# Three reorderings in a fused two-layer decoder step: an exponential step against its consumer, a projection column against a pair of transposes, a copy against a square

## The chip, the cores and the metric

The kernel runs on one NeuronCore of a Trainium2 chip. The metric is the device time of one execution in microseconds, as a median over executions. The engines are TensorE (PE: matmuls; PEld: its weight loads), VectorE (DVE), ScalarE (ACT), GpSimd (POOL) and SyncE (SP, which issues most transfers). Each works through its own instructions in order; between engines only semaphores order the work.

## The reference

One step of a two-layer decoder trunk for a prompt of 256 tokens and 8 samples of 4 tokens (288 columns in all, model width 1024), in float32. The three places that the change touches compute this:

```
# layer 0, Mamba-2 scan, chunks of 128 tokens
a_cs = cumsum(dt * A);  decay_in = exp(where(causal, a_cs[q] - a_cs[k], -inf))
y_diag = einsum(C.B, decay_in, x*dt);  y_off = einsum(C, h_prev, exp(a_cs))
y = (y_diag + y_off + x * d_skip) * silu(z)
# layer 1, RWKV-7 mixer
r, k, v = xr @ wr, xk @ wk, xv @ wv
kk = k * kk_coef;  kk = kk / max(sqrt(sum(kk*kk)), 1e-12)      # per head of 64
S = S * w_t + (S a_t) b_t^T + v_t k_t^T;  y_t = S r_t           # here in chunks, by a triangular inverse
```

Around them lie the attention of layer 0, its feed-forward part, and the mixture of experts of layer 1 (8 experts, top 2).

## The kernel before

Activations lie feature-major, as 8 tiles of 128 features by 288 tokens. Each engine has its program written out by hand; weights stream through a ring of three slots, which SP fills again when the last reader has signalled. The eight PSUM banks are dealt out in the order of `stage` calls: stage number modulo 8 is the bank, and a bank is taken again when its last reader has signalled `bank_free`. Two lists set the order of the work, and all engines walk over the same list: `first` (calls of `l0`, from line 418) for the layer-0 mixer, and `core` (calls of `step`, from line 531) for the RWKV core. Each engine does its own share of an item and passes over items in which it has none.

**Items of `first` around the change.** The 16 heads of the scan go in four quads. `EA q`: DVE writes the arguments of the decays into two buffers `Eb` (8 `tensor_scalar`, line 1681), ACT takes their exponentials (1123, 1129). `EM q`: DVE multiplies them by the C.B product (1697), copies the ends of the decays (1700) and multiplies by C (1701), which signals `cs_ready`. `Y q`: PE does 24 small matmuls (12 into each of two banks), then DVE drains each bank in two instructions (1726, 1727). `Z t` is a column of the z projection: 8 float32 matmuls with 288 columns, each of which shows in the trace as two passes; ACT applies silu (1075). `EA q` from q = 2 on overwrites buffers that `Y q-2` reads, and so waits on DVE for both banks of `Y q-2` to be full.

**The key columns of layer 1.** PE does column `Rk t` (8 matmuls), then for t > 0 the matmul `KN t-1` (one float32 matmul, which sums squares over heads). ACT copies column t into `k1` (line 1286) and squares the scaled keys of tile t-1 (line 1282), which signals `kksq_ready`, for which `KN t-1` waits. DVE makes those scaled keys from the copy (1933, `kk_raw`), and has a scan and four more instructions per tile. This loop is not in a list: PE's part is the loop over `column` and `squared_norm`, ACT's the loop at line 1279.

**Items of `core` around the change.** `Rv t` is a column of the value projection (copied out by ACT, line 1313), `BO t` one matmul for the bonus term, `X 0` the first product of the triangular systems (DVE masks it at line 1994 and signals POOL, which masks rows at line 935), `M0 0` two masked copies and two additions of the identity on DVE (2003, 2005), half by half, each half signalling `m0_ready`. `T 0,0,q` are four transposes of half q on PE (2777), which wait for `m0_ready`; ACT copies them (1313); `LY 0,1,q` and `LM 0,1,q` are the first level of the inverse.

Of the kernel before, what the change touches and what calls it, by code (L numbers as in the profile page):

```python
# [10 lines left out]
ACT = mybir.ActivationFunctionType  # L11
# [117 lines left out]
def decoder_trunk(nc, a, out):  # L129
    with ExitStack() as ctx:  # L130
# [5 lines left out]
        def sem(name):  # L136
            if name not in sems:
                sems[name] = ctx.enter_context(nc.semaphore(name))
            return sems[name]
# [42 lines left out]
        def area(n):  # L182
            o = pos[0]
            pos[0] += n
            assert pos[0] <= ARENA, (pos[0], ARENA)
            return ar[:, o:o + n]
# [77 lines left out]
        vT = area(KT * T).rearrange("p (k t) -> p k t", t=T)  # L264
# [6 lines left out]
        cum, pinv = [ar[:, A4_at + i * KT * T:A4_at + (i + 1) * KT * T].rearrange("p (k t) -> p k t", t=T) for i in range(2)]  # L271
# [134 lines left out]
        def stage(name, n):  # L406
            assert name not in base
            base[name] = order[0]
            order[0] += n
# [6 lines left out]
        def l0(name, *which):  # L416
            first.append((name, which))
            stage((name, *which), SIZES.get(name, 1))
# [22 lines left out]
        l0("EA", 1)  # L441
        l0("Z", 3)
        l0("EM", 0)
        l0("EA", 2)
        l0("Y", 0)
        l0("Z", 4)
        l0("EM", 1)
        l0("EA", 3)
        l0("Y", 1)
        l0("Z", 5)  # L450
        l0("EM", 2)
        l0("Y", 2)
# [89 lines left out]
        def step(name, *which):  # L542
            core.append((name, which))
            n = {"X": 2, "A": 2, "M0": 0, "sA": 4, "sX": 2, "sZ": 2, "sU": 2, "sM": 0, "sE": 0, "WP": 0}.get(name, 1)
            stage((name, *which), n)
# [15 lines left out]
        step("M0", 0)  # L561
        step("Rv", 5)
        step("BO", 4)
        step("Rv", 6)
        step("T", 0, 0, 0)
        step("T", 0, 0, 1)
        step("BO", 5)
        for g in range(4):
            for lv in range(1, 6):
# [89 lines left out]
        def bank(g):  # L659
            return ps[:, g % 8, :]  # L660

        def full(eng, g):

            eng.wait_ge(sem(f"bank_full{g % 8}"), g // 8 + 1)
# [4 lines left out]
        def freesem(g):  # L669
            return sem(f"bank_free{g % 8}")  # L670
# [70 lines left out]
        def _(sp):  # L741
# [7 lines left out]
            def load_ffn_down(c):  # L749
# [3 lines left out]
                sp.dma_start(ring[:, o + GU:o + SLOT], a["ffn_w"][c][:, GU:SLOT]).then_inc(sem(f"ffn_down_loaded{c % RING}"), 16)  # L753

            for n, (name, _, src, w) in enumerate(items):
                if n == 0:
                    continue
# [260 lines left out]
        def _(act):  # L1018
            A = nc.scalar.activation
# [58 lines left out]
            for name, which in first:  # L1078
# [57 lines left out]
                elif name in ("K", "Q"):  # L1136

                    t = which[0]
# [105 lines left out]
            def own_share(n):  # L1244

                mrow = (1, 4, 5, 2, 0, 3)[n]
                full(act, users[n - 2])
                for k in range(KT):
                    if n == 2:
                        act.wait_ge(sem("h_tile"), KT + k + 1)  # L1250
                    A(xi[n % 2][:, k, :], h[:, k, :], ACT.Copy, scale=ommu[:, 8 * mrow + k:8 * mrow + k + 1]).then_inc(sem("act_tile"), 1)  # L1251
# [25 lines left out]
            lora_out("g", gT, None)  # L1277
            load_functions(LN_EXP)
            for t in range(KT + 1):
                if t:  # L1280
                    act.wait_ge(sem("kk_raw"), t)
                    A(pinv[:, t - 1, :], vT[:, t - 1, :], ACT.Square).then_inc(sem("kksq_ready"), 1)
                if t < KT:
                    g = base[f"Rk{t}"]
                    full(act, g)
                    A(k1[:, t, :], bank(g)[:, 0:T], ACT.Copy).then_inc(freesem(g), 1)
            own_share(5)
            act.wait_ge(sem("kn_max"), KT)
            for t in range(KT):
# [25 lines left out]
            for name, which in core:  # L1315
                g = base[(name, *which)]
                if name == "Rv":
                    t = which[0]
# [32 lines left out]
                elif name == "LY":  # L1351
                    q = which[2]
                    out_of(g, Yi[:, 4 * q:4 * q + 4, :], bank(g).rearrange("p (h t) -> p h t", t=P))
                    if which[0] == 0 and which[1] > 1:
                        t = 2 * (which[1] - 2) + q
# [139 lines left out]
        def _(dve):  # L1495
# [476 lines left out]
            for name, which in core:  # L1972
# [88 lines left out]
                elif name == "GV":  # L2061
                    n = which[0]
                    ks, ts, _, rsd = gn_unit(n)
                    emptied(dve, base["GM", n])
                    dve.wait_ge(sem("head_rs"), 18 + n + 1)
# [1179 lines left out]
```

## Time and profile before

| | before |
|---|---|
| time of the runs | 1682.03 us median of 3 (1681.26 to 1684.17) |
| the profiled execution | 1684.17 us, span 1682.5 us |
| PE, PEld busy | 1647.9 us (98%), 1369.8 us (81%) |
| DVE, ACT, POOL busy | 1172.3 us (70%), 914.9 us (54%), 145.0 us (9%) |
| granted TensorE clock | 0.991 of full |

The span is the time from the first to the last instruction. Float32 matmuls of 288 columns start every 0.24 us per pass when nothing holds PE. The layer-0 mixer ends near 300 us, its feed-forward part near 505 us, the mixer of layer 1 near 900 us; the experts take the rest. In a timeline row the columns are start, duration (of a merged row: from the start of its first to the end of its last instruction), engine, line, operation, output and inputs, shape, count, and in brackets the idle time before it and what ended it. A merged PE row can seem to overlap the next one: ends of matmuls are modelled.

### The profile page before, as it was taken

The numbers are of one execution on the slowest core, as the hardware profiler recorded it, in microseconds if no ns is written. First come the engines' busy times: TensorE is split into PE (matmuls) and PEld (weight loads), VectorE is DVE, ScalarE is ACT, GpSimd is POOL, SyncE is SP. The second block draws the span as 40 slices with busy tenths as digits, with TensorE's granted clock in tenths as the row PEclk, the third lists the DMA queues.
The fourth block names the chain that finished last, engine by engine and source line by source line (L and its number), as shares of the span: only waits on it lengthen the run. The fifth ranks groups of instructions, "written<-read, shape, count | busy, mean of one in ns | idle before, by whom it ended". The sixth has DMA issues, their size and how long they took to land.

```text
span 1682.5 us, 25536 instructions
## 1 busy us (share of the span) xinstructions
PE 1647.9 (98%) x9976; PEld 1369.8 (81%) x9976; DVE 1172.3 (70%) x1512; ACT 914.9 (54%) x1190; POOL 145.0 (9%) x180
## 2 busy tenths in 40 slices
PE   9989899999999999999999999999999999999999
PEld 7766687999997778998867887878788787878787
DVE  4653823766667645443556979798887979898897
ACT  3352622533427425333425767687776767687774
POOL 1104000000000023222032000000000000000101
PEclk9999989999999999999899999999999999999999
DMA  8922443544323220000156989798997979898993
GB/s 345 388 100 108 201 162 139 225 151 156 145 100 140 101 100 1 2 2 2 58 200 240 426 335 427 315 418 356 378 410 319 429 307 424 349 384 350 380 426 130
DMA packets 41096, 405.02 MB, mean 241 GB/s; under 512 B 4784, under 2 KB 5072, under 8 KB 11664
## 3 DMA queue, kind: packets, MB, share of 16 engines
q1 hardware_dynamic: 34336, 372.64, 54.9%
q0 software_dynamic: 6672, 31.14, 4.6%
q8 instruction: 63, 1.03, 0.2%
q14 instruction: 25, 0.20, 0.0%
HBM read 379.49 MB, written 26.30 MB: 241 GB/s over the span
## 4 chain that ended last, share of the span: by engine, by line
PE 91%; DVE 4%; ACT 2%; issue 1%; DMA 1%; POOL 0%; DVEq 0%; ACTq 0%; SPq 0%; POOLq 0%
PE ps L2317 87%; DVE rest_ring L2124 1%; DMA ring<-in_moe_w 1%; PE ps L3089 1%; PE ps L2777 1%; PE ps L2725 1%; DVE arena L1668 0%; ACT arena L1251 0%; ACT arena L1264 0%; DVE arena L1681 0%; PE ps L3042 0%; PE ps L2519 0%; DVE arena L1756 0%; POOL ring L924 0%; DVE arena L1542 0%
## 5 line engine op out<-in xcount | busy, mean ns | idle before, releaser
L2317 PE MATMUL ps<-head,hsel 128*128 128x512 f32 x1408 | 458.1, 397 | 2.8 <-DVE rest_ring L2124 2.8
L2317 PEld LDWEIGHTS ps<-head,hsel 128*128 128x128 f32 x1408 | 264.5, 188 | 61.4 <-DVE rest_ring L2124 7.8
L2124 DVE TENSOR_TENSOR rest_ring<-ring,head 128x2048 fp32r<-128x2048 f32 x128 | 291.1, 2285 | 14.1 <-ACT head L1403 14.0
L2317 PE MATMUL ps<-arena,ring 128*128 128x288 f32 (+9 forms) x1408 | 256.6, 347 | 1.2 <-ACT arena L1257 1.2
L1403 ACT ACTIVATE head<-ring 128x2048 fp32r<-128x2048 f32 x128 | 243.2, 1913 | 20.5 <-DMA ring<-in_moe_w 20.5
L2317 PEld LDWEIGHTS ps<-arena,ring 128*128 128x128 f32 (+4 forms) x1408 | 199.8, 189 | 52.8 <-issue 7.7
L2317 PE MATMUL ps<-rest_ring,hsel 128*128 128x512 f32 x512 | 199.8, 390 | 0.0
L2317 PE MATMUL ps<-head,actT_split 128*128 128x512 f32 x512 | 169.1, 394 | 6.8 <-issue 5.6
L2317 PE MATMUL ps<-rest_arena,head 128*128 128x288 f32 x704 | 174.8, 296 | 0.0
L2317 PE MATMUL ps<-rest_arena,rest_ring 128*128 128x288 f32 x528 | 155.7, 295 | 0.0
L2317 PE MATMUL ps<-h,ring 128*128 128x288 f32 (+2 forms) x624 | 133.5, 371 | 1.8 <-DVE h L1513 1.8
L2317 PEld LDWEIGHTS ps<-h,ring 128*128 128x128 f32 (+2 forms) x624 | 99.6, 176 | 35.5 <-issue 9.1
L2317 PEld LDWEIGHTS ps<-rest_arena,head 128*128 128x128 f32 x704 | 122.6, 188 | 0.1
L2317 PEld LDWEIGHTS ps<-head,actT_split 128*128 128x128 f32 x512 | 96.2, 188 | 30.9 <-issue 8.3
L2118 DVE TENSOR_TENSOR rest_ring<-ring,head 128x2048 fp32r<-128x2048 f32 x48 | 109.7, 2285 | 9.7 <-ACT head L1398 9.7
L2317 PE MATMUL ps<-arena 64*64 64x64 f32 (+11 forms) x1194 | 100.8, 283 | 13.0 <-DVE arena L1701 5.3
L2124 DVE TENSOR_TENSOR rest_arena<-arena,head 128x1024 fp32r<-128x1024 f32 (+1 forms) x64 | 110.4, 1752 | 1.7 <-ACT head L1403 1.6
L2317 PEld LDWEIGHTS ps<-rest_ring,hsel 128*128 128x128 f32 x512 | 96.5, 188 | 18.2
L2317 PE MATMUL ps<-hsel,head 128*128 128x288 f32 x352 | 103.9, 295 | 0.0
L1579 DVE TENSOR_TENSOR x<-x,ps 128x288 f32<-128x288 f32 x110 | 48.2, 452 | 78.0 <-PE ps L2317 77.6
L1403 ACT ACTIVATE head<-arena 128x1024 fp32r<-128x1024 f32 (+1 forms) x64 | 92.5, 1485 | 15.4 <-DMA arena<-in_moe_w 15.1
L2317 PE MATMUL ps<-rest_ring,actT_split 128*128 128x512 f32 x256 | 99.7, 390 | 0.0
(387 smaller groups left out, 2471.4 us busy)
## 6 DMA issues: line engine op xcount, KB each, us to landing
ring<-in_moe_w SPq DMA_DIRECT2D x64, 2048.0 KB, 12.2
ring<-in_moe_w SPq DMA_DIRECT2D x64, 1024.0 KB, 8.1
arena<-in_moe_w SPq DMA_DIRECT2D x24, 2048.0 KB, 11.2
arena<-in_moe_w SPq DMA_DIRECT2D x24, 1024.0 KB, 7.4
ring<-in_ffn_w SPq DMA_DIRECT2D x11, 2048.0 KB, 7.6
ring<-in_ffn_w SPq DMA_DIRECT2D x11, 1024.0 KB, 4.9
moe_rows<-arena POOLq DMA_DIRECT2D x1, 6656.0 KB, 34.1
ring<-in_w_in SPq DMA_DIRECT2D x2, 3072.0 KB, 13.2
```

The costliest lines, as they stand in the source:

```text
L1403: A(mhead[c % 2][:, o:o + w], mslot[s][:, o:o + w], ACT.Copy).then_inc(sem("gu_head"), 1)
L1579: V.tensor_tensor(x[:, m, :], x[:, m, :], bank(g)[:, 0:T], ALU.add).then_inc(freesem(g), 1)
L2118: V.tensor_tensor(mrest[s][:, GU:SLOT], mslot[s][:, GU:SLOT], down_head(c).bitcast(F32), ALU.subtract).then_inc(sem("dn_split"), 1)
L2124: V.tensor_tensor(mrest[s][:, o:o + w], mslot[s][:, o:o + w], mhead[c % 2][:, o:o + w].bitcast(F32), ALU.subtract).then_inc(sem("gu_split" ...
L2317: return nc.tensor.matmul(o, l, r, start=start, stop=stop, skip_group_check=skip)
L2725: ins = nc.tensor.transpose(b[0:rows, i * P:(i + 1) * P], src[:, 4 * hf + i, t0:t0 + rows], ident)
L2777: ins = nc.tensor.transpose(b[:, n * P:(n + 1) * P], (Mi if lv else Mti)[gg % 2][:, 4 * q + n, :], ident)
L3089: ins = nc.tensor.transpose(turned(c)[:, u * P:(u + 1) * P], actm[c % 2][:, u * P:(u + 1) * P], ident)
```

## The change

Three orders are changed; no instruction is added, removed or altered.

```
@@ layer-0 list
         l0("EM", 0)
+        l0("Y", 0)
         l0("EA", 2)
-        l0("Y", 0)
         l0("Z", 4)
         l0("EM", 1)
+        l0("Y", 1)
         l0("EA", 3)
-        l0("Y", 1)
@@ core list
         step("BO", 4)
-        step("Rv", 6)
         step("T", 0, 0, 0)
         step("T", 0, 0, 1)
+        step("Rv", 6)
         step("BO", 5)
@@ ScalarE, key columns
             for t in range(KT + 1):
-                if t:
-                    act.wait_ge(sem("kk_raw"), t)
-                    A(pinv[:, t - 1, :], vT[:, t - 1, :], ACT.Square).then_inc(sem("kksq_ready"), 1)
                 if t < KT:
                     g = base[f"Rk{t}"]
                     full(act, g)
                     A(k1[:, t, :], bank(g)[:, 0:T], ACT.Copy).then_inc(freesem(g), 1)
+                if t:
+                    act.wait_ge(sem("kk_raw"), t)
+                    A(pinv[:, t - 1, :], vT[:, t - 1, :], ACT.Square).then_inc(sem("kksq_ready"), 1)
```

In the first, PE's own order does not change (`EA` has no PE work and no bank), nor does ACT's; on VectorE the draining of `Y 0` and `Y 1` (lines 1726, 1727) goes ahead of the arguments of `EA 2` and `EA 3` (line 1681). VectorE at that place, the difference:

```order
 L1700 COPY arena<-arena 128x4
 L1701 TENSOR_TENSOR arena<-arena 128x512
-L1681 TENSOR_SCALAR arena<-arena 128x128 x8
 L1726 SCALAR_TENSOR_TENSOR rs<-arena,vec,ps 128x256
 L1727 TENSOR_TENSOR arena<-arena,rs 128x256
 L1726 SCALAR_TENSOR_TENSOR rs<-arena,vec,ps 128x256
 L1727 TENSOR_TENSOR arena<-arena,rs 128x256
+L1681 TENSOR_SCALAR arena<-arena 128x128 x8
 L1697 TENSOR_TENSOR arena<-arena 128x512 x2
```

The eight argument instructions of `EA 2` moved behind the four of `Y 0`; the same happens once more for `EA 3` and `Y 1`.

In the second, TensorE's transposes `T 0,0,0` and `T 0,0,1` (line 2777) go ahead of the column `Rv 6` (8 matmuls from `arena,ring`). The banks of the three swap with them, and ScalarE copies the transposes out before the column. TensorE at that place, the difference:

```order
 L2317 MATMUL ps<-arena,ring 128x288 x8
 L2317 MATMUL ps<-arena,cst 128x288
+L2777 MATMUL ps<-cst,ring 128x128 x8
 L2317 MATMUL ps<-arena,ring 128x288 x8
-L2777 MATMUL ps<-cst,ring 128x128 x8
 L2317 MATMUL ps<-arena,cst 128x288
 L2317 MATMUL ps<-ring 128x128 x8
```

The first two rows are `Rv 5` and `BO 4`, the last two `BO 5` and `LY 0,1`. The transposes moved from behind to ahead of `Rv 6`.

In the third, ScalarE's order in the key columns. Before, from the table load on; line 1286 is the copy of column t, line 1282 the square of tile t-1:

```order
L1049 ACT_TABLE_LOAD
L1286 ACTIVATE arena<-ps 128x288
L1282 ACTIVATE arena<-arena 128x288
L1286 ACTIVATE arena<-ps 128x288
L1282 ACTIVATE arena<-arena 128x288
```

The same place now, where line 1283 is the copy and line 1286 the square:

```order
L1049 ACT_TABLE_LOAD
L1283 ACTIVATE arena<-ps 128x288 x2
L1286 ACTIVATE arena<-arena 128x288
L1283 ACTIVATE arena<-ps 128x288
L1286 ACTIVATE arena<-arena 128x288
```

Each square moved behind the copy of the next column. TensorE's order there is unchanged: `Rk t`, then `KN t-1`.

## Rows read from the trace of the kernel before

**Rows 1.** The page's busy line and its chain that ended last, by engine
```profile
PE 1647.9 (98%) x9976; PEld 1369.8 (81%) x9976; DVE 1172.3 (70%) x1512; ACT 914.9 (54%) x1190; POOL 145.0 (9%) x180
PE 91%; DVE 4%; ACT 2%; issue 1%; DMA 1%; POOL 0%; DVEq 0%; ACTq 0%; SPq 0%; POOLq 0%
```

**Rows 2.** Timeline, all engines, quads 0 and 1 of the scan
```profile
89.19 1.53 PE L2317 MATMUL ps<-arena 128*64 128x128 f32 x24 [2.15 <-DVE arena L1701]
90.66 4.15 PE L2317 MATMUL ps<-h,ring 128*128 128x288 f32 x16
90.77 1.66 DVE L1681 TENSOR_SCALAR arena<-arena 128x128 f32<-128x128 f32 x8 [1.83 <-PE ps L2317]
92.34 0.47 DVE L1726 SCALAR_TENSOR_TENSOR rs<-arena,vec,ps 128x256 f32<-128x256 f32 x1
...
92.99 0.61 ACT L1129 ACTIVATE arena<-arena 128x512 f32<-128x512 f32 x1
...
94.05 1.28 DVE L1697 TENSOR_TENSOR arena<-arena 128x512 f32<-128x512 f32 x2
...
96.39 1.53 PE L2317 MATMUL ps<-arena 128*64 128x128 f32 x24 [1.59 <-DVE arena L1701]
```

**Rows 3.** Timeline, quads 2 and 3 of the scan
```profile
103.59 1.53 PE L2317 MATMUL ps<-arena 128*64 128x128 f32 x24 [1.59 <-DVE arena L1701]
...
104.51 0.48 DVE L1726 SCALAR_TENSOR_TENSOR rs<-arena,vec,ps 128x256 f32<-128x256 f32 x1 [1.17 <-PE ps L2317]
...
106.21 1.28 DVE L1697 TENSOR_TENSOR arena<-arena 128x512 f32<-128x512 f32 x2
...
109.13 1.53 PE L2317 MATMUL ps<-arena 128*64 128x128 f32 x24
```

**Rows 4.** Timeline, key columns, one of seven like periods
```profile
544.77 0.65 PE L2317 MATMUL ps<-arena,cst 128*128 128x288 f32 x2
544.97 0.41 ACT L1286 ACTIVATE arena<-ps 128x288 f32<-128x288 f32 x1 [2.52 <-PE ps L2317]
...
545.89 0.44 ACT L1282 ACTIVATE arena<-arena 128x288 f32<-128x288 f32 x1 [0.51 <-DVE arena L1933]
...
549.14 0.65 PE L2317 MATMUL ps<-arena,cst 128*128 128x288 f32 x2
```

**Rows 5.** Timeline, layer 0: a square from ACT releases a sum over heads
```profile
184.61 0.39 ACT L1144 ACTIVATE arena<-ps 128x288 f32<-128x288 f32 x1
...
184.90 0.39 ACT L1145 ACTIVATE arena<-ps 128x288 f32<-128x288 f32 x1
...
185.34 0.30 PEld L2317 LDWEIGHTS ps<-arena,cst 128*128 128x128 f32 x2 [0.62 <-ACT arena L1145]
185.34 0.75 PE L2317 MATMUL ps<-arena,cst 128*128 128x288 f32 x2 [0.17 <-ACT arena L1145]
```

**Rows 6.** Timeline, value columns and the first transposes
```profile
629.97 4.04 PE L2317 MATMUL ps<-arena,ring 128*128 128x288 f32 x16
630.23 1.47 DVE L2005 TENSOR_TENSOR ring<-ring,cst 128x512 f32<-128x512 f32 x1
...
632.93 0.69 DVE L2005 TENSOR_TENSOR ring<-ring,cst 128x512 f32<-128x512 f32 x1
...
633.85 1.04 PE L2777 MATMUL ps<-cst,ring 128*128 128x128 f32 x8
...
635.21 2.00 PE L2317 MATMUL ps<-ring 128*128 128x128 f32 x16
```

**Rows 7.** Windows, PE alone: stretch, length, busy (count), granted clock, DMA share, GB/s
```profile
90.00:110.00 20.00, 16.82 (x126) 1.00 0.46 185
185.00:191.00 6.00, 2.46 (x16) 1.00 0.82 315
...
248.00:252.00 4.00, 4.00 (x10) 0.58 0.95 344
```

**Rows 8.** Timeline, PE: twelve output columns, the lowered clock at their start
```profile
247.88 48.52 PE L2317 MATMUL ps<-arena,ring 128*128 128x288 f32 x192
```

**Rows 9.** Waits of SP's own queue: waiter, releaser, us in total, times, longest
```profile
SPq L811 <- PE ps L2317: 544.6, 77, 10.8
```

More of the change, by code:

```diff
@@ L443, in decoder_trunk @@
         l0("EM", 0)
+        l0("Y", 0)
         l0("EA", 2)
-        l0("Y", 0)
         l0("Z", 4)
         l0("EM", 1)
+        l0("Y", 1)
         l0("EA", 3)
-        l0("Y", 1)
         l0("Z", 5)
@@ L563, in decoder_trunk @@
         step("BO", 4)
-        step("Rv", 6)
         step("T", 0, 0, 0)
         step("T", 0, 0, 1)
+        step("Rv", 6)
         step("BO", 5)
@@ L1279, in _ @@
             for t in range(KT + 1):
-                if t:
-                    act.wait_ge(sem("kk_raw"), t)
-                    A(pinv[:, t - 1, :], vT[:, t - 1, :], ACT.Square).then_inc(sem("kksq_ready"), 1)
                 if t < KT:
@@ L1286, in _ @@
                     A(k1[:, t, :], bank(g)[:, 0:T], ACT.Copy).then_inc(freesem(g), 1)
+                if t:
+                    act.wait_ge(sem("kk_raw"), t)
+                    A(pinv[:, t - 1, :], vT[:, t - 1, :], ACT.Square).then_inc(sem("kksq_ready"), 1)
             own_share(5)
```

## The prediction

> **What bounds the kernel now.** I read the page first: TensorE is busy 98% of the span and has 91% of the chain that ended last [rows 1]. So microseconds are won or lost only where TensorE waits, and each move is judged by one question: does TensorE start its next instruction earlier or later? I then read the timeline at the three places.
>
> In the scan TensorE does wait. `Y 0` starts at 89.19, and `Y 1` at 96.39 after 1.59 us of idling for VectorE's line 1701; `Y 2` follows at 103.59 in the same way [rows 2, 3]. The period of 7.20 us is a ring through VectorE. In the key columns TensorE does not wait at all: `KN` matmuls start at 544.77 and 549.14, a period of 4.37 us that is nothing but matmul passes [rows 4]. Around the first transposes it does not wait either: `Rv 6` starts at 629.97, the transposes at 633.85 (3.88 us later, sixteen passes), `LY` at 635.21 [rows 6].
>
> **Part 1, the scan (a gain).** I take the ring apart. Before: from `Y 0` on TensorE (89.19) VectorE waits 1.58 us until both banks are full, starts the arguments of `EA 2` at 90.77 and spends 1.57 us on them; the drain of `Y 0` starts at 92.34 and takes 1.71; `EM 1` starts at 94.05, and 2.34 later `Y 1` starts on TensorE [rows 2]. 1.58 + 1.57 + 1.71 + 2.34 = 7.20.
>
> After: the drain comes first, and its first instruction needs only the first of the two banks. Quad 2 shows how soon that is, since VectorE is waiting there: `Y 2` starts at 103.59 and the drain at 104.51, 0.92 us later; it ends at 106.21, 1.70 us later [rows 3]. So the new ring is 0.92 + 1.70 + 1.57 + 2.34 = 6.53 us, 0.67 less. It is run through twice, to `Y 1` and to `Y 2`: 1.34 us. From `Y 2` to `Y 3` the period is 5.54 us and is made of TensorE's own work (the row of `Y 3` names no wait) [rows 3]; the new ring there would be 0.92 + 1.70 + 2.34 = 4.96, still shorter, so nothing more is gained and nothing given back.
>
> The cover for the moved edit: the arguments of `EA 2` now start at about 91.8 instead of 90.77, and the exponentials behind them, the last of which started at 92.99 [rows 2], end about a microsecond later, near 94.7. `EM 2` asks for them only near 99.9. ScalarE's silu of `Z 4` slips by that microsecond too; its reader is the drain of `Y 2` near 103. If that cover went, the gain would go with it, so the term lies between -1.34 and 0. I take -1.3.
>
> **Part 2, the key columns (a loss).** `KN t-1` needs the square of tile t-1. Before, that square ran right behind VectorE's scaled keys, at 545.89 for the `KN` that TensorE reaches at 549.14: 3 us of slack [rows 4]. Now the square stands behind the copy of column t, and that copy cannot start before TensorE has finished column t, which is just when TensorE arrives at `KN t-1`. ScalarE's copy starts at 544.97, 0.20 us after the present start of `KN` [rows 4]. The square can start 0.29 behind it (184.61 to 184.90, two of ScalarE's instructions in a row) and takes 0.44 (line 1282) [rows 4, 5]. TensorE follows 0.05 after the end of such a square (184.90 + 0.39 = 185.29, matmul at 185.34), and its two passes then take 0.75 rather than 0.65, since the weights were not loaded ahead [rows 4, 5]. Sum: 0.20 + 0.29 + 0.44 + 0.05 + 0.10 = 1.08 us. There are seven such matmuls, `KN 0` to `KN 6`; the eighth comes after another column, with its square long done. 7 x 1.08 = 7.6 us.
>
> Behind the waiting matmul stand the next key column and, on VectorE, the maximum of the norms; both have slack only against TensorE, so nothing catches up. Bounds: with a square of 0.39 and the weights loaded ahead, 0.93 each, 6.5 in all; with the square starting only when the copy of 0.41 is done, and 0.25 us from release to matmul as in the scan, 0.20 + 0.41 + 0.44 + 0.25 + 0.10 = 1.40 each, 9.8 in all.
>
> On the weights the trace and a rule can be set side by side. In layer 0 the weight load of the released matmul starts at 185.34, with it and not before it, although its weights are a constant table [rows 5]. The Trainium skill (TensorE: Matmul & The Clock Gate, "What happens when you issue a matmul") says that TensorE's queue can pull weight loads ahead of matmuls in flight. By that rule the 0.10 would go, and the term would be 6.9. The row is against it here, and I leave the 0.10 in.
>
> **Part 3, the transposes (a loss).** They wait for `m0_ready`. VectorE's two signals come at 630.23 + 1.47 = 631.70 and 632.93 + 0.69 = 633.62 [rows 6]. Nothing in the change makes VectorE or POOL earlier: the product `X 0` and the masks keep their places. TensorE is through with `BO 4` at 629.97. Before, `Rv 6` filled exactly the time until 633.85, when both halves were ready. Now TensorE idles until about 631.9, does the first four transposes, idles again, does the second four at 633.85 as before, and only then begins `Rv 6`. The eight transposes take 0.87 us together, so four of them 0.44: `Rv 6` starts at 634.3 and ends at 638.2, `BO 5` takes 0.49, `LY` starts at 638.7 instead of 635.21. That is 3.88 (the column) less 0.44 (the half done earlier) = 3.4 to 3.5. Queued behind are `Rv 6`, `BO 5`, `LY`, and through `BO 5` VectorE's last bonus products and POOL; all of them slide with TensorE. What the earlier copies of the transposes give back is the wait of `LY`, a few tenths at most. Bounds: 3.1 (0.3 given back) and 3.9 (the whole column late). I take 3.5.
>
> **Sum.** -1.3 + 7.6 + 3.5 = +9.8 us. The profiled execution took 1684.17 us (span 1682.5, 1.67 around it) and would take 1694.0. It was the slowest of the three; on the median, 1682.03, the same sum gives 1691.8, which I round to 1692. The bounds of the terms give +8.3 to +13.7.
>
> **Rivals.**
>
> *The clock falls behind the split wait.* Between 630 and 634.3 TensorE would do 0.4 us of work. The nearest rows: at 185 to 191 it was busy 2.46 of 6 us and the clock stayed at 1.00; at 248 to 252, after a stretch of very small matmuls, it was granted 0.58, which lies between the levels of 1.2 and 2.4 GHz [rows 7]. What a fall costs: the 192 passes from 247.88 took 48.52 us where sixteen take 3.88, so 46.6: 1.9 us [rows 6, 8]. Result 1693.7. The new gap is emptier than any of those rows. The Trainium skill (TensorE: Matmul & The Clock Gate, "Why this matters for your kernels") advises against long idle gaps between bursts of matmuls, because the clock then goes back to the half rate; by that rule this case happens in some executions. The key columns are no such place: with 1.08 idle in 5.45 they are as busy as the scan (16.82 of 20 at 1.00) [rows 7].
>
> *The transposes are ready sooner.* VectorE's first addition takes 1.47 beside POOL's work and the second 0.69 alone [rows 6]. If the new order freed VectorE of that contention, its four instructions would take 2.8 us from 628.6, the second signal would come at 631.4, and the term would be about 1.2 instead of 3.5: 1689.5. Against it: POOL starts on the same signal as before.
>
> *The end is set by the expert weights (not slower).* If the stream of expert weights were the bound, a later TensorE would only find fuller slots, and parts 2 and 3 would be swallowed: about 1681 to 1682. The point on which this turns is who waits for whom in the expert stage: SP waits for TensorE to free a slot 77 times, 544.6 us in all [rows 9], so the loads follow TensorE and slide with it.
>
> *The squares do not hold TensorE.* If the order on ScalarE did not reach TensorE, part 2 would be nothing: 1684.3. Only a slack of over a microsecond between column and `KN` would allow it, and there is none: they are 0.24 apart.
>
> **How the numbers follow.** Forecast as summed 0.70; clock 0.12; transposes sooner 0.08; weights set the end 0.05; squares harmless 0.03; some gain that I do not see 0.02. A measurement of this kernel tells about 0.2%, 3.4 us, from no change: slower 0.90, same 0.08, faster 0.02. The range runs from 1687.5, which takes in the case at 1689.5 and a median that lies 2 us low, to 1696, which takes in the upper bound of +13.7.
>
> **What would show it.** (1) `Y 1` and `Y 2` start after waits of about 0.9 us instead of 1.6, and `Y 3` 1.3 earlier than 109.13. (2) The key columns have a period of 5.45 instead of 4.37, and the page of waits has a new line of seven waits of TensorE for the square, of about 0.8 to 1 us each. (3) TensorE waits twice before the transposes, 3.4 us in all, and `LY` comes about 3.5 later against `BO 4`. I would be wrong in the main if the key columns kept their period, or if TensorE's waits in the expert stage shrank by as much as it arrives late.

## The result, and the profile after

| | before | after |
|---|---|---|
| time of the runs, same chip | 1684.17 us median of 5 (1681.26 to 1685.12) | 1697.47 us median of 5 (1694.51 to 1703.20) |
| ratio | | 1.008 [1.0056, 1.0103] |
| the profiled execution | 1684.17 us, span 1682.5, clock 0.991 | 1697.79 us, span 1696.2, clock 0.987 |

The change makes the kernel 13.3 us slower. The direction was forecast and the size was not: 1697.47 lies 1.5 us above the range that ended at 1696. Over all 23 executions of the changed kernel, those of `after_again` below among them, the median is 1696.6, still above it. The page of the changed kernel, busy line and chain, answers to [rows 1]. TensorE is busy longer although its instructions are the same: a first sign that some of them ran at a lower clock.

```profile
PE 1656.4 (98%) x9976; PEld 1372.8 (81%) x9976; DVE 1172.4 (69%) x1512; ACT 914.6 (54%) x1190; POOL 142.8 (8%) x180
PE 90%; DVE 5%; ACT 2%; issue 1%; DMA 1%; POOL 0%; DVEq 0%; ACTq 0%; SPq 0%; POOLq 0%
```

The waits of PE and of SP's queue (waiter, releaser, us in total, times, longest). The first two lines are new, the third stood at 5.3 before; SP still waits for TensorE 77 times, as in [rows 9].

```profile
PE ps L2317 <- ACT arena L1286: 5.8, 7, 0.8
...
PE ps L2777 <- DVE ring L2005: 2.9, 2, 1.6
...
PE ps L2317 <- DVE arena L1701: 4.0, 3, 2.1
...
SPq L811 <- PE ps L2317: 543.9, 77, 10.8
```

**The scan.** Timeline of the four quads, all engines, answering to [rows 2, 3]. The drain starts 0.92 behind `Y 0`, the argument instructions stand behind it, and the period is 6.54 instead of 7.20, twice; the third stays 5.54.

```profile
89.84 1.53 PE L2317 MATMUL ps<-arena 128*64 128x128 f32 x24 [2.15 <-DVE arena L1701]
...
90.76 0.48 DVE L1726 SCALAR_TENSOR_TENSOR rs<-arena,vec,ps 128x256 f32<-128x256 f32 x1 [1.17 <-PE ps L2317]
...
92.47 1.65 DVE L1681 TENSOR_SCALAR arena<-arena 128x128 f32<-128x128 f32 x8
...
96.38 1.53 PE L2317 MATMUL ps<-arena 128*64 128x128 f32 x24 [0.93 <-DVE arena L1701]
...
102.92 1.53 PE L2317 MATMUL ps<-arena 128*64 128x128 f32 x24 [0.93 <-DVE arena L1701]
...
108.46 1.53 PE L2317 MATMUL ps<-arena 128*64 128x128 f32 x24
```

**The key columns.** Timeline, answering to [rows 4]; line 1283 is the copy, 1286 the square. The copy starts at 546.27, the square 0.31 later, `KN` when the square is done, and the next one 5.46 us on instead of 4.37.

```profile
546.27 0.41 ACT L1283 ACTIVATE arena<-ps 128x288 f32<-128x288 f32 x1 [3.47 <-PE ps L2317]
546.58 0.43 ACT L1286 ACTIVATE arena<-arena 128x288 f32<-128x288 f32 x1
...
547.06 0.30 PEld L2317 LDWEIGHTS ps<-arena,cst 128*128 128x128 f32 x2 [1.29 <-ACT arena L1286]
547.07 0.75 PE L2317 MATMUL ps<-arena,cst 128*128 128x288 f32 x2 [0.83 <-ACT arena L1286]
...
552.53 0.75 PE L2317 MATMUL ps<-arena,cst 128*128 128x288 f32 x2 [0.83 <-ACT arena L1286]
```

**The transposes.** Timeline of PE, answering to [rows 6]: `BO 4`, the two halves of transposes, `Rv 6`, `BO 5`, `LY`. Besides the two waits, look at the duration of `Rv 6`: sixteen passes took 4.04 before and take 6.56 now.

```profile
638.47 0.65 PE L2317 MATMUL ps<-arena,cst 128*128 128x288 f32 x2
640.73 0.66 PE L2777 MATMUL ps<-cst,ring 128*128 128x128 f32 x4 [1.62 <-DVE ring L2005]
642.66 1.11 PE L2777 MATMUL ps<-cst,ring 128*128 128x128 f32 x4 [1.27 <-DVE ring L2005]
643.57 6.56 PE L2317 MATMUL ps<-arena,ring 128*128 128x288 f32 x16
649.97 0.65 PE L2317 MATMUL ps<-arena,cst 128*128 128x288 f32 x2
650.45 1.95 PE L2317 MATMUL ps<-ring 128*128 128x128 f32 x16
```

Windows of PE (stretch, length, busy, granted clock, DMA share, GB/s) give the reason, and answer to [rows 7]: behind the waits the engine was granted the lower of its two levels, 1.2 instead of 2.4 GHz. The first three rows are another such place, in attention, which the prediction did not name: the stretch at 185 to 191 in [rows 7] had stayed at 1.00.

```profile
188.00:190.00 2.00, 1.25 (x6) 0.50 1.05 455
...
192.00:194.00 2.00, 1.27 (x14) 0.50 0.94 406
...
198.00:200.00 2.00, 2.00 (x10) 0.98 1.05 455
...
640.00:642.00 2.00, 0.66 (x4) 0.96 0.00 0
642.00:644.00 2.00, 1.34 (x5) 0.50 0.00 0
...
648.00:650.00 2.00, 2.00 (x9) 0.84 0.00 0
```

**Where the 13.7 us between the two spans lie.** I cut both timelines of PE at the same instructions. The gather is the expert stage's first step, 48 matmuls that start at 900.11 before.

| stretch | before | after | difference |
|---|---|---|---|
| start to `Y 0` | 89.19 | 89.84 | +0.65 |
| `Y 0` to `Y 3` | 19.94 | 18.62 | -1.32 |
| `Y 3` to `Rk 0` (attention, feed-forward) | 423.90 | 425.87 | +1.97 |
| `Rk 0` to `X 0` (key columns) | 91.38 | 99.06 | +7.68 |
| `X 0` to `LY` (transposes) | 10.80 | 17.06 | +6.26 |
| `LY` to the gather of the expert stage | 264.90 | 263.21 | -1.69 |
| gather and experts, to the end | 782.39 | 782.54 | +0.15 |

The first row is not the change's: in the fourteen profiles of this study `Y 0` starts between 88.52 and 90.05, whatever was edited behind it. The -1.69 is one fall of the clock fewer, at 844 to 850, that the profile of before had. The +1.97 and a part of the +6.26 are additional falls.

The mean granted clock of an execution translates into time: at two levels, one half of the other, the time at the lower one is 2 x (1 - clock) x span. For before 2 x 0.009 x 1682.5 = 30 us, for after 2 x 0.013 x 1696.2 = 44 us. Executions of one kernel differ mainly in this mean. 93 executions of the kernel before lie at 1681.7 on the mean where the clock was 0.993 (15 of them), at 1683.3 for 0.991 to 0.992 (48), at 1685.3 for 0.989 to 0.990 (4) and at 1690.1 for 0.986 to 0.988 (26).

### The profile page after: what moved, and what is told of

It reads as the page before. It is cut to its first block, busy times and chain, and to the rows that moved or that the text cites. A ratio compares the mean times of both kernels' runs of the same rounds, so it can differ in the third digit from the quotient of the medians.

```text
span 1696.2 us, 25536 instructions
## 1 busy us (share of the span) xinstructions
PE 1656.4 (98%) x9976; PEld 1372.8 (81%) x9976; DVE 1172.4 (69%) x1512; ACT 914.6 (54%) x1190; POOL 142.8 (8%) x180
## 4 chain that ended last, share of the span: by engine, by line
PE 90%; DVE 5%; ACT 2%; issue 1%; DMA 1%; POOL 0%; DVEq 0%; ACTq 0%; SPq 0%; POOLq 0%
PE ps L2317 86%; DVE rest_ring L2124 1%; DMA ring<-in_moe_w 1%; PE ps L3089 1%; PE ps L2777 1%; PE ps L2725 1%; DVE arena L1668 0%; ACT arena L1251 0%; DVE arena L1681 0%; ACT arena L1264 0%; PE ps L3042 0%; PE ps L2519 0%; DVE arena L1756 0%; POOL ring L924 0%; DVE arena L1542 0%
## 6 DMA issues: line engine op xcount, KB each, us to landing
ring<-in_w_in SPq DMA_DIRECT2D x2, 3072.0 KB, 13.1
```

## The experiments

The theory after the result: the three waits cost what was forecast, and the rest, some 3 to 4 us, is clock that falls at the new waits and in attention. The rival: the sum of the waits is itself wrong, or the whole costs a fixed 13 that has nothing to do with the clock. Kernels of one table or paragraph ran on one chip, beside the executions of before that are named there. The added matmuls of some kernels ("fillers") are float32 products of two constant tables into a bank that is about to be overwritten; they change no result and let TensorE work where it would wait.

### Each part alone

`scan_only` (order `Y 0`, `EA 2`, `Z 4`, `EM 1`, `Y 1`, `EA 3`), `keys_only` (square behind the copy), `transposes_only`:

```
 scan_only:        +l0("Y", 0)  l0("EA", 2) -l0("Y", 0)   and the same for Y 1, EA 3
 keys_only:        the two blocks of ScalarE's loop exchanged
 transposes_only:  -step("Rv", 6)  step("T",0,0,0)  step("T",0,0,1)  +step("Rv", 6)
```

> Part 1 alone: VectorE drains Y 0 and Y 1 before the arguments of EA 2 and EA 3. All theories: TensorE's waits before Y 1 and Y 2 are 0.93 us instead of 1.59, and Y 3 starts 1.32 us earlier against Y 0. Theory A (the excess over the forecast comes from the emptied stretch before the transposes): the time is 1.3 us below the kernel before, and the clock around 186 to 198 falls no more often than before. Rival B (the excess comes from the attention stretch at 186 to 198, which the earlier start of part 1 moves into a fall of the clock): the clock falls to half there for some 10 us in the profile, 2 us are lost, and the time is 0 to 1 us above the kernel before.

> Part 2 alone: ScalarE squares tile t-1 only after copying column t. All theories: seven waits of TensorE for line 1286 of 0.83 us and a period of 5.46 us instead of 4.37, no fall of the clock in the key columns. Theory A: +7.7 us over the kernel before. Rival C (the waits themselves cost more downstream than they last): +9 us or more.

> Part 3 alone: the first transposes go ahead of column Rv 6. Theory A: two waits of TensorE of 1.6 and 1.3 us, and behind them Rv 6 takes 6.4 us instead of 3.9, because the clock is granted at half in that stretch; LY starts about 6 us later against BO 4, and the time is +5 to +6.5 us where that happens, +3.5 where it does not. Rival B (the clock there is chance of one profile): Rv 6 takes 3.9 us, the time is +3.5 us.

Measured, beside 35 executions of before (median 1684.20, mean 1685.35):

| | median of 12 | ratio [95%] | mean less before's |
|---|---|---|---|
| scan_only | 1683.93 | 0.9996 [0.9980, 1.0012] | -1.1 |
| keys_only | 1690.48 | 1.0042 [1.0023, 1.0060] | +6.5 |
| transposes_only | 1688.82 | 1.0031 [1.0012, 1.0049] | +4.7 |

In the traces the first two terms are as forecast: `Y 0` to `Y 3` 18.61 (-1.33), the key columns 99.07 (+7.69, with no clock in it). The times of keys_only say the same at equal clocks: at 0.992 its executions have 1690.4 (7) and those of before 1682.7 (12), 7.7 apart; the 9 us of the rival are not there. For the transposes `X 0` to `LY` takes 15.75, +4.95. That is neither the 6 that was expected with a fall nor the 3.5 without one: the fall came, but the lower level lasted 3.4 us and not 6.8. The timeline of PE in transposes_only shows the same two waits and `Rv 6` longer by half as much as in the changed kernel:

```profile
631.64 0.66 PE L2777 MATMUL ps<-cst,ring 128*128 128x128 f32 x4 [1.62 <-DVE ring L2005]
633.58 1.11 PE L2777 MATMUL ps<-cst,ring 128*128 128x128 f32 x4 [1.27 <-DVE ring L2005]
634.49 5.25 PE L2317 MATMUL ps<-arena,ring 128*128 128x288 f32 x16
```

In times the three add up to +10.1 by the means, +10.6 by the medians. For the scan alone no gain can be told from nothing; its profile has the fall in attention that rival B asked for, but 3.4 us long and not 10.

### Filling the split wait

`transposes_filled` is transposes_only with three fillers before the first and two before the second half of the transposes; `all_filled` is the changed kernel with the same five; `after_again` is the changed kernel once more, beside it.

```
+ if gg == 0:
+     for _ in range(3 - q):
+         mm(b[:, 0:T], C("blk64"), cst[:, 0:T])
  pe.wait_ge(sem("m0_ready"), 2 * gg + q + 1)
```

> Part 3 alone, with five float32 matmuls of 288 columns of a constant table put in front of the transposes' waits (three before the first, two before the second; they write the bank that the transposes overwrite). They take 2.4 us of a wait of 2.9. Theory A: TensorE is kept at work, the clock stays at 1.00, Rv 6 takes 3.9 us, and the time is +3.5 us over the kernel before, 2 to 3 us less than part 3 without them. Rival B: the same time as part 3 without them, within 0.5 us.

> The changed kernel once more, beside new runs of the kernel before. Theory A (waits add 9.8 to 10 us, falls of the clock add a part that differs from execution to execution): the fastest executions of both kernels lie 9.8 us apart, the means 10.5 to 12.5, and the profile loses clock at places where other kernels of this study lose it too (186 to 200, before Rv 6, about 905), not where nothing was lost before. Rival (a fixed cost of 13 us that the forecast lacked): the fastest executions lie 13 us apart too.

> The changed kernel with the five matmuls of a constant table in front of the waits of the first transposes. Theory A: Rv 6 takes 3.9 us instead of 6.4, LY starts 8.6 us after the end of BO 4's start instead of 12, and the mean is 1 to 2.5 us below the changed kernel's, still 9 to 11 above the kernel before. Rival (the fall before Rv 6 only moves one that would come later): the mean is the same as the changed kernel's within 0.7 us.

Timeline of PE in transposes_filled. The waits have shrunk to 0.16 and 0.29, the transposes still start when VectorE lets them, and `Rv 6` is back at 4.05:

```profile
631.34 0.66 PE L2781 MATMUL ps<-cst,ring 128*128 128x128 f32 x4 [0.16 <-DVE ring L2005]
631.83 1.14 PE L2317 MATMUL ps<-cst 128*128 128x288 f32 x4
633.26 0.65 PE L2781 MATMUL ps<-cst,ring 128*128 128x128 f32 x4 [0.29 <-DVE ring L2005]
633.75 4.05 PE L2317 MATMUL ps<-arena,ring 128*128 128x288 f32 x16
```

`X 0` to `LY` is 14.12 here and 14.13 in all_filled, against 17.06 and 17.08 in the two profiles of the changed kernel. So the wait term by itself is 14.12 - 10.80 = 3.32, and the fall adds 2.94 (`Rv 6` 2.5, the second half of the transposes 0.4). Without fillers `Rv 6` was slowed in 3 of 3 profiles, with them in 0 of 2.

The times don't follow, and by the means both expectations came out as their rivals had it. transposes_filled: median 1689.76, mean 1690.2, against 1688.82 and 1690.1 without fillers. all_filled: 1695.67 median of 6, after_again 1696.02 median of 6 (ratios 1.0072 [1.0046, 1.0099] and 1.0073 [1.0045, 1.0100] to the 1682.69 of 23 executions of before beside them), means 1697.3 and 1697.7. The profile of all_filled has no fall before `Rv 6`, but one at 842 to 848 that the first profile of the changed kernel lacks: 41 us at the lower level in all against 44. Of the 2.93 us that it gains before `LY` it loses 1.67 there (264.88 from `LY` to the gather against 263.21), and its expert stage is 0.6 longer. And transposes_filled was profiled in a slower execution of 1694.03, with a fall at the gather of the expert stage; the gather of 48 matmuls, in transposes_filled and then in the kernel before:

```profile
903.00 12.99 PE L2317 MATMUL ps<-arena 128*128 128x128 f32 x48 [1.23 <-ACT arena L1434]
```

```profile
900.11 8.48 PE L2317 MATMUL ps<-arena 128*128 128x128 f32 x48 [1.23 <-ACT arena L1434]
```

There 13.6 us lie at the lower level between 904 and 920, and between the clocks 0.987 and 0.991 lie 2 x 0.004 x 1684 = 13.5. So a fall of this kind would fit the executions of before near 1690; that it is this one is not shown, since none of them was profiled.

The rival of a fixed 13 had a test, the fastest executions, and in after_again's own six that test goes the rival's way: 1694.50 against 1681.41, 13.1 apart, and the means 13.0. But that execution had a clock of 0.990. With all 23 executions of the changed kernel and the 93 of before, the means are 1697.1 and 1685.1, 12.0 apart, and at equal clocks the distance is smaller: 9.6 at 0.993 (a single execution, 1691.33, against 1681.7), 8.3 at 0.991 (2), 7.4 at 0.987 (4 against 21). None is near 13, and the first is the sum of the three waits (7.68 + 3.32 - 1.32 = 9.68). So the fixed 13 falls, by few executions at the top.

### The scan, further

TensorE's waits between the quads of the scan can be removed altogether. `scan_ahead` makes the products of quad 1 before quad 0 is drained; `scan_ahead_warm` adds two fillers in the wait before the expert stage's gather, near 899; `scan_ahead2` brings `EM 3` ahead of `Y 2` too. `EA 2` and `EA 3` still follow the `Y` whose buffers they overwrite.

```
 before:      EM0 EA2 Y0 Z4 EM1 EA3 Y1 Z5 EM2 Y2 EX Z6 EM3 CM
 scan_ahead:  EM0 EM1 Y0 EA2 Z4 Y1 EM2 EA3 Z5 Y2 EX Z6 EM3 CM
 scan_ahead2: EM0 EM1 Y0 EA2 Z4 Y1 EM2 EA3 Z5 EM3 Y2 EX Z6 CM
```

> A longer step in the direction of part 1, and nothing of parts 2 and 3: VectorE does EM 1 ahead of draining Y 0 and EM 2 ahead of EA 3 (order EM 0, EM 1, Y 0, EA 2, Y 1, EM 2, EA 3, Y 2). TensorE's waits before Y 1 and Y 2 vanish, the periods from Y 0 to Y 1 to Y 2 to Y 3 are 5.5 us each, and Y 3 starts 3.3 us earlier against Y 0 than before. Theory A: the fastest executions and the mean are 2.5 to 3.3 us below the kernel before. Rival (the gain is eaten by the clock, or by ScalarE's table loads between exponentials and silus, which now follow closer): less than 1.5 us.

> The same, and two float32 matmuls of 288 columns of a constant table in the wait of 1.2 us before the expert stage's gather (near 899). In one profile of this study the clock stood at half from 904 to 920 and cost about 6 us, and a third of the executions of the kernel before lie 6 us above the others. If that wait decides it, the slow group (6 us above) goes, and the mean is 1.5 to 2 us below the version without them. Rival (the transposes and small matmuls ahead of the wait decide it): the slow group stays.

> The longer step of part 1, with EM 3 also ahead of the draining of Y 2, which in the version before it waited 1.9 us on VectorE for the silu of Z 5 behind ScalarE's table loads. Expected: three periods of 5.54 us from Y 0 to Y 3, 16.6 in all against 19.94 before, 3.3 us gained by waits; of that 0 to 2 us lost again where the clock falls in the attention, so a mean of 1.5 to 3.3 us below the kernel before. Rival (all is lost to the clock again): within 1 us of the kernel before.

In scan_ahead `Y 0` to `Y 3` takes 18.03: two periods of 5.53 and 5.54, then one of 6.96. VectorE's and ScalarE's timelines show why. `Y 2` starts at 100.21; the second bank of its drain waits for the silu of `Z 5`, which stands behind a table load, so the products for `Y 3` are late:

```profile
101.65 0.42 DVE L1727 TENSOR_TENSOR arena<-arena,rs 128x256 f32<-128x256 f32 x1
103.96 0.48 DVE L1726 SCALAR_TENSOR_TENSOR rs<-arena,vec,ps 128x256 f32<-128x256 f32 x1 [1.89 <-ACT arena L1075]
...
102.17 1.28 ACT L1075 ACT_TABLE_LOAD   x1
103.46 0.41 ACT L1075 ACTIVATE arena<-ps 128x288 f32<-128x288 f32 x1
```

In scan_ahead2 that is gone; PE's timeline names no wait behind `Y 0`, and the four quads take 16.62 instead of 19.94:

```profile
89.82 1.53 PE L2317 MATMUL ps<-arena 128*64 128x128 f32 x24 [2.15 <-DVE arena L1701]
...
95.36 1.53 PE L2317 MATMUL ps<-arena 128*64 128x128 f32 x24
...
100.90 1.53 PE L2317 MATMUL ps<-arena 128*64 128x128 f32 x24
...
106.44 1.53 PE L2317 MATMUL ps<-arena 128*64 128x128 f32 x24
```

Times: scan_ahead 1684.10 and scan_ahead_warm 1684.29, medians of 12 (ratios 0.9991 [0.9975, 1.0007] and 0.9996 [0.9983, 1.0009]); the means are 1683.8 and 1683.7 against 1684.7, so 1 us lower where theory A had 2.5 to 3.3: its rival came out. None of the 12 executions of scan_ahead_warm is near 1690, but only one of scan_ahead's 12 is, so what the wait before the gather does (filled from 1.23 to 0.26 us) is not settled. scan_ahead2 1681.02 against 1684.09, 0.9989 [0.9972, 1.0005]: the lowest median of all kernels here, with a mean 3.2 lower (1681.8 against 1685.0), but its interval still holds 1. Compared at equal clocks the gain is there: at 0.993 its executions have 1678.4 (2) against before's 1681.7, at 0.987 1687.2 (3) against 1690.3 (21), so 3.0 to 3.3 us, which is what the trace says. The comparison is fair only where the falls stand in like places: scan_ahead's six executions at 0.988 have 1684.4 against 1689.4, 5.0 us, while its trace has gained 1.9.

### Does the scan's gain come back in attention?

A fall at 186 to 200 stands in 6 of the 6 profiles so far whose scan was changed (scan_only, after, after_again, all_filled, scan_ahead, scan_ahead_warm). With the old scan it stands in 1 of 4 profiles, transposes_filled. In four of the six it makes `Y 3` to `Rk 0` 2.0 us longer, in scan_only 1.6. In scan_ahead_warm and transposes_filled that stretch is not longer, but only because another fall is missing: their twelve output columns have none at their start and take 46.83 instead of the 48.52 of [rows 8]. The row is scan_ahead_warm's:

```profile
248.11 46.83 PE L2317 MATMUL ps<-arena,ring 128*128 128x288 f32 x192
```

Measured from `Y 3` to the start of these columns, the fall in attention costs something every time: 138.75 us in the kernel before, 140.30 in scan_only, scan_ahead_warm and transposes_filled (lower level for 3.4 us), 140.69 in the changed kernel (10.2 us). Is it the earlier arrival, or the gaps in attention themselves? `scan_delayed` is scan_only with three fillers (1.46 us) before the first attention column. `attention_filled` is before with three fillers in each of three waits of attention; `scan_ahead2_filled` is scan_ahead2 with the same nine.

```
+ if which[0] == 0:            # scan_delayed: in K 0
+     for _ in range(3): mm(take(g)[:, 0:T], C("blk64"), cst[:, 0:T])
+ if j == 2:                   # attention_filled: before the wait of S 2;
+     for _ in range(3): mm(take(g)[:, 0:T], C("blk64"), cst[:, 0:T])
                               # the same with j == 0 in PT 0 and in O 0
```

> Part 1 alone, with three float32 matmuls of 288 columns of a constant table on TensorE in front of the first K column (1.46 us), so that everything behind comes at about the time that it has in the kernel before. All six profiles of kernels with a changed scan show the clock at half in some part of 186 to 200, and one of four with the old scan. Theory P (the gain of part 1 moves the attention's waits in time, and the fall follows from when they come): no fall from 186 to 198 in the profile, and the times fall into the groups of the kernel before (1682, 1684, 1690), mean within 1 us of it. Rival (the falls there are chance and have nothing to do with part 1): falls as often as with part 1 alone, mean 1.4 us above part 1 alone.

> The kernel before, with three such matmuls in each of the three waits of 1.7 to 2.0 us of the attention (before the first transposes of the probabilities, the first outputs and the third scores; nine in all, 4.4 us of 5.4). Theory: TensorE is kept at work there, the clock never falls from 184 to 200, and the executions near 1684 (a clock mean of 0.988 to 0.991) move to 1682, so the mean is about 1 us lower; the group near 1690 stays. Rival (the waits there were harmless): the same mean as the kernel before within 0.5 us, or above it where the fillers delay the work behind them.

> The same with the nine matmuls in the attention's waits. If the falls there come from the waits, they go: the time from the start of Y 3 to the first LoRA key column (423.9 us in the kernel before, 425.9 with a fall) is 424, and the mean is 3 to 4 us below the kernel before. If they come from something else, the mean equals that of the version without them.

| | median of 12 | ratio [95%] | `Y 0` to `Y 3` | `Y 3` to `Rk 0` | expert stage to the end |
|---|---|---|---|---|---|
| before (profile) | 1684.09 of 35 | | 19.94 | 423.90 | 773.98 |
| scan_delayed | 1685.67 | 1.0014 [0.9997, 1.0030] | 18.63 | 425.28 | 775.11 |
| attention_filled | 1685.19 | 1.0016 [0.9999, 1.0033] | 19.94 | 423.86 | 776.23 |
| scan_ahead2 | 1681.02 | 0.9989 [0.9972, 1.0005] | 16.62 | 423.83 | 773.98 |
| scan_ahead2_filled | 1684.21 | 0.9996 [0.9977, 1.0014] | 18.25 | 422.15 | 776.74 |

(The last column starts at the end of the gather. In scan_delayed 1.46 of `Y 3` to `Rk 0` are its fillers; in scan_ahead2_filled the clock fell at 88 to 94, in the scan itself, and one fall of the others, at 244 to 250, is missing.) None of the four has a fall at 186 to 200. For the two with fillers in the gaps that speaks for the gaps; but scan_ahead2 has every gap of attention open, comes 2.7 us earlier than before, and doesn't fall either. Windows of PE in scan_ahead2, busy as little as 0.13 of 2 us and at 1.00:

```profile
186.00:188.00 2.00, 0.62 (x6) 1.00 1.06 455
188.00:190.00 2.00, 1.53 (x24) 1.00 1.08 467
190.00:192.00 2.00, 0.13 (x2) 1.00 1.00 430
```

The same in scan_only, whose attention comes some 2 us later than that; there the clock falls behind the empty window:

```profile
190.00:192.00 2.00, 1.48 (x24) 1.00 1.11 479
192.00:194.00 2.00, 0.05 (x2) 1.00 1.06 455
194.00:196.00 2.00, 1.92 (x16) 0.78 0.97 418
196.00:198.00 2.00, 2.00 (x6) 0.50 0.94 397
```

So the gaps do not settle whether the fall comes: with them open it came in 7 of 12 profiles, with them filled in 0 of 2, and scan_only and scan_ahead2 differ there only in when they arrive. With one profile of each kernel I can't tell a rule from chance, and that the faster scan brings the fall is not shown. That the scan's gain is always given back is refuted by scan_ahead2. The times bore out none of the theories: the means of scan_delayed and of attention_filled are 1.5 above the kernel before, where within 1 and 1 below were expected, and scan_ahead2_filled's is 0.8 below it instead of 3 to 4, and 2.4 above scan_ahead2.

Filling attention cost time elsewhere. The expert stage is 1.1 us longer with three fillers (scan_delayed) and 2.2 and 2.8 with nine. In all_filled, too, the longest wait for nothing that the profile shows is 1.5 instead of 0.8. Waits of PE in attention_filled, where `issue` stood at 6.8 for 11 waits, the longest 0.8, in the kernel before:

```profile
PE ps L2317 <- issue: 8.0, 12, 1.7
...
PE ps L2317 <- DVE actT_split L2282: 2.3, 3, 1.0
```

Between 1300 and 1350 a wait for nothing that the profile shows is 1.7 long instead of 0.8, and at 933 stands a wait of 1.05 for VectorE's line 2282 that scan_ahead2 doesn't have there. Together they are most of the 2.2 us by which the expert stage is longer. At a clock of 0.993 the executions agree: 1683.8 (6) against 1681.7. Eighteen passes added at 186 to 195 us were paid for 740 us later and more; by what way is open.

## Why the prediction was off

The direction, the places and the mechanisms of all three parts held: the sum of the waits was forecast at 9.8 and measured 9.68. The size of the whole did not hold.

**Part 1** was forecast at -1.34 by the ring and measured -1.32, in steps of 0.92 to the drain and 0.93 of wait as written. The cover held: the later exponentials made nobody late.

**Part 2** was forecast at seven times 1.08 = 7.6 and measured 7.68. Each wait is 0.83, and the released matmul takes 0.75 instead of 0.65 as in [rows 5]; its weight load starts at 547.06, with it (547.07). In the Trainium skill (TensorE: Matmul & The Clock Gate, "What happens when you issue a matmul") weight loads can be pulled ahead of matmuls in flight; behind these waits for a semaphore the seven pairs lost the 0.10 all the same.

**Part 3** was forecast at 3.4 to 3.5 and its waits measured 3.32 (transposes_filled). `Rv 6` was put 4.8 us behind the start of `BO 4` (629.5 to 634.3); it comes 4.7 behind it in transposes_filled, and 5.1 in the changed kernel, where the second half of the transposes already runs at the lower clock. The 0.2 between 3.5 and 3.32 is the second half: it was put where it stood before, 4.37 behind `BO 4` (633.85), and comes 4.19 behind it, as soon as its signal allows.

**The failed step** is the first rival, "The clock falls behind the split wait". It got a chance of 0.12 and a price of 1.9 us, and the forecast put the clock at nothing. In the profiles it was the rule, not the exception: 3 of 3 where the wait was open. Its price was 2.94 and 2.96 in the two profiles of the changed kernel, where the lower level lasted 6.8 us, and 1.6 in transposes_only (15.75 less 14.12), where it lasted 3.4. I had read from [rows 7] that a stretch busy 2.46 of 6 us stayed at 1.00, and concluded that this one would stay too, although I wrote myself that it was emptier than any row. (The 0.4 us of work from 630 to 634.3 is a slip: both halves lie in it, 0.87 by the prediction's own figure.) And I had priced the fall by [rows 7, 8], about 3.4 us at the lower level. For a fall of that length the price was about right: the same columns without it took 46.83, so it costs 1.7. But the fall in the changed kernel was twice as long. The Trainium skill's advice against idle gaps between bursts of matmuls (same page, "Why this matters for your kernels") points the way these three profiles go, although it speaks of long gaps and the two here are 1.62 and 1.27 us, with four transposes between them; scan_ahead2's attention, with its gaps at 1.00, shows that a gap alone does not decide.

**The second omission** belongs to the same step: only the new gap was asked about. The fall in attention, +1.97 in the profile, is in old code 80 us behind part 1, and is more than that part's gain of 1.32. Whether part 1 brought it is open: transposes_filled, with the old scan, has one too. scan_only's time, a ratio of 0.9996 with an interval of 0.16% on either side, fits a gain mostly given back, and would also fit the full 1.3.

**The base.** The sum was put on the median of three, 1682.03. Beside the changed kernel, the median of before was 1684.17. On that base +9.8 gives 1694.0, so 2.1 of the 5.7 us between 1691.8 and 1697.5 are chance in the base. The remaining 3.5 us are what the profiled spans show as 13.7 - 9.7 = 4.0: +2.94 and +1.97 and -1.69 of clock, +0.65 at the start, +0.15 at the end. Over all executions it is less, 12.0 - 9.7 = 2.3 us, with a mean clock of 0.988 against 0.990: 2 x 0.0119 x 1695 = 40 us at the lower level against 2 x 0.0098 x 1684 = 33.

**The other rivals.** The transposes were not ready sooner: the second half is released 4.19 us behind the start of `BO 4`, and VectorE's two additions take 1.46 and 0.69 as before. The experts did not set the end: SP's waits shrank by 0.7 of 544.6, and the stage moved as a whole. The squares did hold TensorE, seven times.

**Open.** Filling the split wait removes the fall in the traces, but saves not one microsecond in the medians (6 and 12 executions, spread over 9 to 11 us). So that the clock before `Rv 6` costs 2.9 us is shown in profiles and not in times. Three explanations are left: falls then come elsewhere, as in all_filled's profile; the fillers cost something in later stages, as in attention_filled; or the profiled executions were lucky. The mean clocks, 0.9897 with fillers against 0.9892 without, differ by less than their scatter and do not decide.

## What to carry to other kernels

Where TensorE sets the end, an order that makes it wait costs the wait, and that part can be worked out to a tenth of a microsecond from starts and durations of the old trace; but put the clock behind a gap that is emptier than any row into the range, from nothing up to half of the time at the lower level, with lengths of more than one fall, and not as an unlikely rival. Before a change of a few microseconds is judged, split the executions by granted clock and compare like with like, after a look at where the falls stand: here the groups lie 8 us apart, and scan_ahead2's 3.2 us, with an interval that holds 1, agree with the trace in each group that both kernels have. To gain in such a scan, look for the products of the next quad that an engine can make before it drains this one, and then at what the drain itself waits for.

## What the runs showed of the hardware

- The same 48 matmuls of the gather took 8.48 us at the full level and 12.99 with most of them at the lower one.
- A fall costs half of its length where TensorE works throughout, and less where it would wait anyway: 3.4 us at the lower level at the start of the output columns cost 1.69 (48.52 against 46.83), 6.8 before `LY` cost 2.94, and 10.2 in attention cost 1.97.
- Identical code ran with a fall in one profile and without one in another (attention in scan_only, and 2.2 us earlier in scan_ahead2).
- Nine added float32 matmuls that fitted into waits (`Y 3` to `Rk 0` stayed at 423.86) lengthened the expert stage by 2.2 us, 0.9 of it as a wait that the profile puts down to issue.
- A weight load of a constant table started with the matmul that waited for a semaphore and not ahead of it: 547.06 and 547.07, and the pair took 0.75 instead of 0.65 us, seven times.
- An ACT_TABLE_LOAD took 1.28 us, and the next instruction on ScalarE started right behind it (102.17, then 103.46).
